# Prompt attention by pairs of heads on row and column halves of the array, with the mask added in VectorE's row reduction

## The chip, the cores and the metric

The kernel runs on one core of one Trainium2 chip. A core has a matrix engine (TensorE, PE in the profile; its weight loads are PEld), a vector engine (VectorE, DVE), a scalar engine (ScalarE, ACT), GpSimd (POOL), SyncE (SP), which issues transfers here, and 16 DMA engines. The metric is the time of one execution on the device in microseconds; lower is better. Before the change three runs took 2658.57, 2660.92 and 2667.46 us.

## The reference, cut to what matters

One step of a hybrid decoder layer over a prompt (1024 tokens) and a sample group (8 sequences of 8 new tokens with 2048 past ones): RMSNorm, one input projection, sparse softmax attention with a token indexer (8 heads of 64), gated DeltaNet (4 heads of 128), output projection, squared-ReLU MLP, final norm. All tensors are float32. The change is in the attention of the prompt:

```
score = sum over indexer heads of relu(qi . ki / 8) * wi, -inf where the key is later than the query
sel   = the 256 highest scores of each query (of its causal keys)
s = q . k / sqrt(64) for the selected keys, else -inf
p = softmax(s);  o = p @ v                     (per head; 8 heads of 64)
```

For queries of the first 256 tokens every causal key is selected.

## The kernel before, in words

The program is a row of stages, each a block in which every engine has its own instruction list, with semaphores between them. Around the change: the indexer and top-256 stages, then the mixer projection, which also turns the top-256 result into masks (one bf16 tile `maskP[t]` of 128 x 128(t+1) per query tile t >= 2, 0 where a key is taken and MASKED = -1e30 elsewhere, L803; `attn_causal` is the causal square, L78) and writes q, scaled by 1/8 (L766), and k transposed to DRAM; conv, gates and the DeltaNet; then `stage_prompt_attention` (L1492), `stage_sample_attention` (L1634), output projection and MLP.

`stage_prompt_attention` works on 64 items, one head h of one query tile t each (t outer, eight heads inner); an item has t+1 key blocks of 128. q, k and v are loaded in three parts (tiles 0 and 1, 2 and 3, 4 to 7) by SyncE, ahead of the first pages for the sample attention; GpSimd loads others of these pages.

The order on each engine is written out by hand:

- TensorE, per item n: `turn(n)`: t+1 transposes of the scaled probabilities into two PSUM banks (L1555); `score(n+2)`: per 512 keys one product of 64 rows (the head's half of the partitions) and one bf16 product of the identity with the mask, which adds the mask in PSUM (L1542, L1544, L1546); `values(n)`: t+1 products with 64 output columns of the array (L1567).
- VectorE: `scale(n+1)`: reciprocal of the row sum and scaling in place (L1619, L1621); `maxes(n+2)`: negated row maximum out of PSUM (L1608); `keep(n)`: the 64 x 128 output of the item into `mix` (L1614).
- ScalarE: copy of the transposed probabilities to SBUF (L1598); `exps(n+2)`: exponential out of PSUM with the row sum (L1588).

Scores of two items lie in four banks, two per item; transposes use two banks, value outputs one each of the last two. A float32 product is two passes, so it is two MATMUL instructions in the trace; a transpose and a bf16 product are one.

Of the kernel before, what the change touches and what calls it, by code (L numbers as in the profile page):

```python
# [58 lines left out]
def constants():  # L59
# [18 lines left out]
    parts["attn_causal"] = MASKED * (col > row)  # L78
# [58 lines left out]
class Kernel:  # L137


    def __init__(self, nc, ctx, a):  # L140
# [28 lines left out]

        self.psI = self.view(m.take(IX_W), IX_W)  # L170
        self.psA = self.view(m.take(3 * AW), 3 * AW)
        self.psC = self.view(m.take(CC), CC)
# [524 lines left out]
def stage_mixer_projection(k):  # L697
# [22 lines left out]
    with nc.Block() as block:  # L720
# [11 lines left out]
        def _(act):  # L732
# [5 lines left out]
            for n, (c, kind, col, wd, at) in enumerate(jobs):  # L738
# [17 lines left out]
                elif c <= V_CHUNK:  # L756
# [9 lines left out]
                    act.activation(stage[i % 4], bank[:, :], ACT.Copy, scale=HD ** -0.5 if c == Q_CHUNK else 1.0).then_inc(kept, 1)  # L766
# [725 lines left out]
def stage_prompt_attention(k):  # L1492
# [6 lines left out]
    m = Map(k.z_at)  # L1499
    prob = [k.view(m.take(SEQ), SEQ) for _ in range(2)]  # L1500
    probT = [k.view(m.take(SEQ), SEQ) for _ in range(2)]
# [3 lines left out]
    items = [(t, h) for t in range(NT) for h in range(H)]  # L1505
# [3 lines left out]
    names = ("scores", "max", "exp", "inv", "scaled", "turned", "kept", "made", "out")  # L1509
    scores, maxed, exped, inverted, scaled, turned, kept, made, out = (k.sem("pa_" + n) for n in names)  # L1510
    n_items = len(items)
    k.stream = PageStream(k)
    with nc.Block() as block:
# [17 lines left out]
        def _(pe):  # L1531
            def score(n):
                t, h = items[n]
                lo = (h % 2) * HD
                if h == 0 and t in first:
                    pe.wait_ge(qk_in[first[t]], 32)
                if n >= 2:
                    pe.wait_ge(exped, n - 1)
                for c in range(0, (t + 1) * P, 512):
                    w = min(512, (t + 1) * P - c)  # L1540
                    bank = k.psum[2 * (n % 2) + c // 512]
                    pe.matmul(bank[:, 0:w], qT[lo:lo + HD, h // 2, t * P:(t + 1) * P], kT[lo:lo + HD, h // 2, c:c + w], start=True, stop=False)  # L1542
                    if t < FIRST_SEL:
                        last = pe.matmul(bank[:, t * P:(t + 1) * P], k.b["ident"], k.b["attn_causal"], start=False, stop=True)  # L1544
                    else:
                        last = pe.matmul(bank[:, 0:w], k.b["ident"], k.maskP[t][:, c:c + w], start=False, stop=True)  # L1546
                last.then_inc(scores, 1)

            def turn(n):
                t, h = items[n]  # L1550
                pe.wait_ge(scaled, n + 1)
                if n:
                    pe.wait_ge(kept, n)
                for j in range(t + 1):
                    last = pe.transpose(k.psum[4 + j // 4][:, (j % 4) * P:(j % 4 + 1) * P], prob[n % 2][:, j * P:(j + 1) * P], k.c["ident"])  # L1555
                last.then_inc(turned, 1)

            def values(n):
                t, h = items[n]
                lo = (h % 2) * HD  # L1560
                if h == 0 and t in first:
                    pe.wait_ge(v_in[first[t]], 16)
                pe.wait_ge(kept, n + 1)
                if n >= 2:
                    pe.wait_ge(out, n - 1)
                for j in range(t + 1):
                    last = pe.matmul(k.psum[6 + n % 2][lo:lo + HD, 0:P], V[:, j, h * HD:(h + 1) * HD], probT[n % 2][:, j * P:(j + 1) * P],  # L1567
                                     start=(j == 0), stop=(j == t))
# [3 lines left out]
            score(1)  # L1572
            for n in range(n_items):
                turn(n)
                if n + 2 < n_items:
                    score(n + 2)
                values(n)

        @block.scalar
        def _(act):  # L1580
            def exps(n):
                t, h = items[n]
                w = (t + 1) * P
                b0 = 2 * (n % 2) * 512
                act.wait_ge(maxed, n + 1)
                if n >= 2:
                    act.wait_ge(turned, n - 1)
                act.activation(prob[n % 2][:, 0:w], k.banks[:, b0:b0 + w], ACT.Exp, bias=stat[:, 0, n:n + 1],  # L1588
                               accum_out=stat[:, 1, n:n + 1]).then_inc(exped, 1)

            exps(0)
            exps(1)
            for n in range(n_items):
                w = (items[n][0] + 1) * P
                act.wait_ge(turned, n + 1)
                if n >= 2:
                    act.wait_ge(made, n - 1)
                act.copy(probT[n % 2][:, 0:w], k.banks[:, 4 * 512:4 * 512 + w]).then_inc(kept, 1)  # L1598
                if n + 2 < n_items:
                    exps(n + 2)  # L1600

        @block.vector
        def _(dve):
            def maxes(n):
                w = (items[n][0] + 1) * P
                b0 = 2 * (n % 2) * 512
# [719 lines left out]
```

## Time and profile before

| | |
|---|---|
| median of three runs | 2660.92 us |
| profiled execution, first to last instruction | 2661.8 us |
| PE busy | 2400.9 us, 90% |
| PEld busy | 1617.1 us, 61% |
| DVE busy | 1399.8 us, 53% |
| ACT busy | 601.4 us, 23% |
| POOL busy | 272.6 us, 10% |

The busy shares are means over the whole program. The page also has the program in 40 slices of 66.5 us; the prompt attention is in the 17th to the 21st. For one stage the stretches, waits and the timeline of that stage are to be read. A matmul's duration includes its way through the array, so durations of matmuls in a row overlap: their pace is read from start to start. "issue" stands for a wait on nothing the profile shows.

### The profile page before, as it was taken

The page shows a single profiled execution, that of the slowest core. Times are in us where ns is not written, and L with a number is a line of the kernel's source. Part 1 is how long each engine was busy: PE and PEld are TensorE (multiplying, and loading weights), DVE is VectorE, ACT ScalarE, POOL GpSimd, SP SyncE. Part 2 cuts the span into 40 slices and gives each one's busy share as a digit, 9 for nine tenths or more (in the row PEclk, how much of TensorE's full clock was granted, in tenths as well). Part 3 has the DMA queues.
Part 4 walks back from the last instruction along what each step waited for, and adds up shares of the span by engine and source line. Part 5 has one row for each costly group of instructions (what it writes and reads, how often), then busy time and mean ns, then how long its engine had stood idle before and what let it go on. Part 6 is the DMA issues. An engine that isn't in the chain of part 4 may idle for free. (4 is left out here: it accounts for less than half of the span.)

```text
span 2661.8 us, 28841 instructions
## 1 busy us (share of the span) xinstructions
PE 2400.9 (90%) x10669; PEld 1617.1 (61%) x10669; DVE 1399.8 (53%) x2208; ACT 601.4 (23%) x1094; POOL 272.6 (10%) x363
## 2 busy tenths in 40 slices
PE   2967999999699987699999999797999999999998
PEld 2522444444258876355654444386888888888887
DVE  3056999999645656534432221265444444444445
ACT  2031442110320101124432111143111211221212
POOL 2221543110020010100000222100000000000000
PEclk9966999999769989559999999898999999999999
DMA  5120001220000001420015674541110110111111
GB/s 142 27 89 1 32 32 48 78 85 12 9 1 1 1 1 33 160 97 1 1 54 180 211 227 128 200 138 53 40 56 32 40 56 32 40 56 32 34 55 68
DMA packets 116152, 171.81 MB, mean 65 GB/s; under 512 B 25784, under 2 KB 66745, under 8 KB 115884
## 3 DMA queue, kind: packets, MB, share of 16 engines
q1 hardware_dynamic: 100140, 124.86, 14.5%
q0 software_dynamic: 15872, 45.11, 5.5%
q8 instruction: 85, 1.39, 0.2%
q14 instruction: 55, 0.45, 0.1%
HBM read 154.02 MB, written 15.91 MB: 64 GB/s over the span
## 5 line engine op out<-in xcount | busy, mean ns | idle before, releaser
L393 PE MATMUL banks<-arena,work 128*128 128x512 f32 x736 | 323.1, 600 | 8.2 <-PEq L292 7.7
L1881 PE MATMUL banks<-h_hi,ml_up_hi 128*128 128x364 f32 (+1 forms) x768 | 253.5, 330 | 8.6 <-DVE ml_up_lo L2217 8.6
L1882 PE MATMUL banks<-h_lo,ml_up_hi 128*128 128x364 f32 (+1 forms) x768 | 253.5, 330 | 0.0
L1883 PE MATMUL banks<-h_hi,ml_up_lo 128*128 128x364 f32 (+1 forms) x768 | 253.4, 330 | 0.0
L393 PEld LDWEIGHTS banks<-arena,work 128*128 128x128 f32 x736 | 140.3, 192 | 186.1 <-issue 186.1
L1881 PE MATMUL banks<-ml_down_hi,ml_hid_hi 128*128 128x512 f32 (+1 forms) x576 | 228.8, 397 | 27.0 <-DVE x L2246 24.5
L524 DVE MATCH_REPLACE8 work<-work 128x384 f32<-128x384 f32 (+6 forms) x224 | 240.0, 1077 | 0.0
L2246 DVE TENSOR_TENSOR x<-x,banks 128x512 f32<-128x512 f32 x256 | 171.5, 685 | 123.3 <-PE banks L1883 123.0
L520 DVE MAX8 work<-work 128x8 f32<-128x384 f32 (+6 forms) x224 | 227.5, 1079 | 0.4 <-PEq L553 0.3
L1882 PE MATMUL banks<-ml_down_lo,ml_hid_hi 128*128 128x512 f32 (+1 forms) x576 | 227.4, 395 | 0.0
L1883 PE MATMUL banks<-ml_down_hi,ml_hid_lo 128*128 128x512 f32 (+1 forms) x576 | 227.0, 394 | 0.0
L2256 DVE TENSOR_TENSOR arena<-arena 128x364 f32<-128x364 f32 (+1 forms) x96 | 51.6, 537 | 209.2 <-ACT arena L2195 209.2
L1881 PEld LDWEIGHTS banks<-h_hi,ml_up_hi 128*128 128x128 f32 x768 | 145.3, 189 | 10.3 <-DVE ml_up_lo L2217 8.8
L1882 PEld LDWEIGHTS banks<-h_lo,ml_up_hi 128*128 128x128 f32 x768 | 145.3, 189 | 0.6
L1883 PEld LDWEIGHTS banks<-h_hi,ml_up_lo 128*128 128x128 f32 x768 | 145.3, 189 | 0.0
L1881 PEld LDWEIGHTS banks<-ml_down_hi,ml_hid_hi 128*128 128x128 f32 (+1 forms) x576 | 106.3, 185 | 58.1 <-DVE x L2246 30.4
L396 PE MATMUL banks<-work,arena 128*128 128x512 f32 (+1 forms) x384 | 124.8, 487 | 0.0
L1883 PEld LDWEIGHTS banks<-ml_down_hi,ml_hid_lo 128*128 128x128 f32 (+1 forms) x576 | 106.3, 185 | 27.0
L1882 PEld LDWEIGHTS banks<-ml_down_lo,ml_hid_hi 128*128 128x128 f32 (+1 forms) x576 | 106.2, 184 | 25.4
L1707 PE MATMUL banks<-work 128*64 128x512 f32 x256 | 116.7, 599 | 0.0
L1542 PE MATMUL banks<-work 64*128 64x512 f32 (+3 forms) x192 | 102.7, 621 | 15.2 <-DMA work<-k_T 15.2
L1743 PE MATMUL banks<-work 128*64 128x512 f32 x256 | 107.7, 611 | 6.9 <-DVE work L1834 6.1
(348 smaller groups left out, 3426.6 us busy)
## 6 DMA issues: line engine op xcount, KB each, us to landing
work<-in_cache_v POOLq DMA_DIRECT2D x128, 256.0 KB, 3.4
work<-in_cache_k SPq DMA_DIRECT2D x128, 256.0 KB, 3.3
arena<-in_w_up SPq DMA_DIRECT2D x32, 512.0 KB, 4.1
arena<-in_w_down SPq DMA_DIRECT2D x32, 512.0 KB, 5.6
work<-in_w_in SPq DMA_DIRECT2D x7, 2048.0 KB, 8.1
op_raw<-in_w_out SPq DMA_DIRECT2D x24, 512.0 KB, 3.5
work<-in_x_prompt SPq DMA_DIRECT2D x8, 512.0 KB, 4.9
x<-in_x_prompt SPq DMA_DIRECT2D x1, 4096.0 KB, 15.3
```

The costliest lines, as they stand in the source:

```text
L393: last = pe.matmul(bank[0:w, :], ring[:, f, col:col + w], hT[:, f, at * 512:(at + 1) * 512], start=(f == 0), stop=(f == KD - 1))
L396: last = pe.matmul(bank[:, 0:w], hT[:, f, at * P:(at + 1) * P], ring[:, f, col:col + w], start=(f == 0), stop=(f == KD - 1))
L520: dve.max(self.best[0:rows, i, :], sc[0:rows, :]).then_inc(self.maxed, 1)
L524: dve.match_replace(sc[0:rows, :], self.best[0:rows, i, :], sc[0:rows, :], TAKEN).then_inc(self.taken, 1)
L1542: pe.matmul(bank[:, 0:w], qT[lo:lo + HD, h // 2, t * P:(t + 1) * P], kT[lo:lo + HD, h // 2, c:c + w], start=True, stop=False)
L1707: last = pe.matmul(rows, qblk[:, (2 * it + b2) * 4 + p, :], kts[n % 2][:, p, :], start=False, stop=(p == 3))
L1743: last = pe.matmul(k.psum[6][b2 * 64:(b2 + 1) * 64, :], PT[:, 4 * c + j, b2 * 64:(b2 + 1) * 64], vp[n % KV_RING][:, j, :], start=(c == 0 a ...
L1881: pe.matmul(out, lh, rh, start=start, stop=False)
L1882: pe.matmul(out, lh, rl, start=False, stop=False)
L1883: return pe.matmul(out, ll, rh, start=False, stop=stop)
L2246: dve.tensor_tensor(part, part, k.psum[4 + n % 4][0:r, :], ALU.add).then_inc(added, 1)
L2256: dve.tensor_tensor(tmp[:, j, 0:w], tmp[:, j, 0:w], tmp[:, j, 0:w], ALU.mult).then_inc(squared, 1)
```

## The change

Heads are taken in pairs, (t, p) with heads 2p and 2p+1. `score` issues, per 512 keys, the product of the even head on rows 0 to 63 and then that of the odd head on rows 64 to 127, into different banks, and no mask product. q is projected with the negated scale and the prompt's masks have the other sign, so scores and masks are negated. VectorE's `mask` adds scores and mask, writes the sum to the SBUF probability tile and takes the row minimum, in one `tensor_tensor_reduce`. ScalarE takes the exponential with scale -1, in place in SBUF. Transposes go to a ring of three banks in chunks of up to 512 keys (banks 4 to 6), each chunk with its own copy on ScalarE. `values` alternates the two heads of the pair on the two column halves, into one bank (7), of which one VectorE copy of 128 x 128 takes both heads. Scores have two sets of banks up to 512 keys, and one set above.

There are as many probability tiles (`prob`) as before, two, but they are now the two heads of one pair, and a pair has no second set; the transposed ones (`probT`) have two sets. `prob` moves over buffers that are done with by then.

```diff
-    parts["attn_causal"] = MASKED * (col > row)
+    parts["attn_causal"] = -MASKED * (col > row)
...
-  act.activation(stage[i % 4], bank[:, :], ACT.Copy, scale=HD ** -0.5 if c == Q_CHUNK else 1.0).then_inc(kept, 1)
+  act.activation(stage[i % 4], bank[:, :], ACT.Copy, scale=-HD ** -0.5 if c == Q_CHUNK else 1.0).then_inc(kept, 1)
...
-  dve.tensor_scalar(masks[i][0:rows, :], sc[0:rows, :], TAKEN, MASKED, ALU.not_equal, ALU.mult)
+  dve.tensor_scalar(masks[i][0:rows, :], sc[0:rows, :], TAKEN, MASKED if i == k.topk.sample else -MASKED, ALU.not_equal, ALU.mult)
...
+    def score_at(n, e):
+        return 512 * (2 * (n % 2) + e if width(n) <= 512 else 2 * e)
...
+            def score(n):                                        # TensorE
+                t, p = pairs[n]
                 ...
+                if width(n) > 512:
+                    pe.wait_ge(masked, 2 * n)
+                elif n >= 2:
+                    pe.wait_ge(masked, 2 * (n - 1))
+                for c in halves(n):
+                    w = min(512, width(n) - c)
+                    for e in range(2):
+                        lo, at = e * HD, score_at(n, e) + c
+                        last = pe.matmul(k.banks[:, at:at + w], qT[lo:lo + HD, p, t * P:(t + 1) * P], kT[lo:lo + HD, p, c:c + w],
+                                         start=True, stop=True)
                 last.then_inc(scores, 1)
+            def turn(n):
+                for e in range(2):
+                    pe.wait_ge(scaled, 2 * n + e + 1)
+                    for c in halves(n):
+                        u = chunk_of[n, e, c]
+                        if u >= NB:                              # NB = 3
+                            pe.wait_ge(kept, u - NB + 1)
+                        for at in range(c, min(c + 512, width(n)), P):
+                            last = pe.transpose(k.psum[4 + u % NB][:, at - c:at - c + P], prob[e][:, at:at + P], k.c["ident"])
+                        last.then_inc(turned, 1)
+            def values(n):
                 ...
+                pe.wait_ge(kept, last_chunk(n, 1) + 1)
                 if n:
+                    pe.wait_ge(out, n)
                 for j in range(t + 1):
+                    for e in range(2):
+                        h = 2 * p + e
+                        last = pe.matmul(k.psum[7][e * HD:(e + 1) * HD, 0:P], V[:, j, h * HD:(h + 1) * HD], probT[n % 2][e][:, j * P:(j + 1) * P],
+                                         start=(j == 0), stop=(j == t))
             score(0)
+            for n in range(n_pairs):
+                if n + 1 < n_pairs:
+                    score(n + 1)
+                turn(n)
+                if n:
+                    values(n - 1)
...
+            def exps(n, e):                                      # ScalarE
+                i, w = 2 * n + e, width(n)
+                act.wait_ge(masked, i + 1)
+                act.activation(prob[e][:, 0:w], prob[e][:, 0:w], ACT.Exp, scale=-1.0, bias=stat[:, 0, i:i + 1],
+                               accum_out=stat[:, 1, i:i + 1]).then_inc(exped, 1)
+            def keep_turned(n):
                 if n >= 2:
                     act.wait_ge(made, n - 1)
+                for e in range(2):
+                    for c in halves(n):
+                        u, w = chunk_of[n, e, c], min(512, width(n) - c)
+                        act.wait_ge(turned, u + 1)
+                        act.copy(probT[n % 2][e][:, c:c + w], k.psum[4 + u % NB][:, 0:w]).then_inc(kept, 1)
                 # order: exps(0, 0), exps(0, 1), then per n: keep_turned(n), exps(n + 1, 0), exps(n + 1, 1)
...
+            def mask(n, e):                                      # VectorE
                 ...
                 dve.wait_ge(scores, n + 1)
+                if n:
+                    dve.wait_ge(turned, last_chunk(n - 1, e) + 1)
+                dve.tensor_tensor_reduce(out=prob[e][:, 0:w], in0=k.banks[:, at:at + w], in1=mask_of[t], scale=1.0, scalar=3.0e38,
+                                         op0=ALU.add, op1=ALU.min, accum_out=stat[:, 0, i:i + 1]).then_inc(masked, 1)
...
+            for n in range(n_pairs):
+                if n + 1 < n_pairs:
+                    for e in range(2):
+                        mask(n + 1, e)
+                    for e in range(2):
+                        scale(n + 1, e)
+                if n:
+                    keep(n - 1)
```

`scale` is as before, with one index per head of a pair. The masks of tiles 0 and 1 are laid out by three small VectorE instructions at the start of the stage.

## Rows read from the trace of the kernel before

**Rows 1.** The page's 40 slices: TensorE's granted clock in tenths of full speed.
```profile
PEclk9966999999769989559999999898999999999999
```

**Rows 2.** Busy times by stretch: length, engines (instructions), clock, DMA share, GB/s.
```profile
1112.44:1127.70 15.26, 14.48 (x44) 8.18 (x45) 7.13 (x30) 5.46 (x23) 6.95 (x13) 0.50 1.03 377
...
1151.50:1185.50 34.00, 34.00 (x93) 16.92 (x91) 11.14 (x32) 9.09 (x24) 0.00 (x0) 0.50 0.00 0
1185.50:1198.70 13.20, 13.20 (x37) 6.71 (x37) 4.07 (x11) 3.40 (x8) 0.00 (x0) 0.50 0.00 1
...
1322.30:1372.10 49.80, 47.26 (x270) 29.84 (x269) 20.04 (x34) 18.64 (x25) 0.00 (x0) 1.00 0.00 1
```

**Rows 3.** Waits in 1100 to 1372 us: who, for whom, total us, times, longest.
```profile
ACT work L1588 <- DVE work L1608: 139.2, 64, 5.1
...
DVE work L1608 <- PE banks L1546: 81.9, 48, 2.6
...
PE banks L1542 <- DMA work<-k_T: 15.2, 1, 15.2
```

**Rows 4.** Timeline of an item of tile 7: start, length, instruction, idle before.
```profile
1340.34 1.11 ACT L1588 ACTIVATE work<-banks,work 128x1024 f32<-128x1024 f32 x1 [3.00 <-DVE work L1608]
...
1340.86 1.09 PE L1555 MATMUL banks<-arena,work 128*128 128x128 f32 x8
...
1341.35 0.19 ACT L1588 ACTIVATION_READ_ACCUMULATOR work<-banks,work 128x1 f32 x1
1341.58 0.16 DVE L1619 RECIPROCAL work<-work 128x1 f32<-128x1 f32 x1 [0.31 <-ACT work L1588]
1341.78 0.75 DVE L1621 TENSOR_SCALAR work<-work 128x1024 f32<-128x1024 f32 x1
...
1341.89 1.12 PE L1542 MATMUL banks<-work 64*128 64x512 f32 x2
...
1342.94 0.39 PE L1546 MATMUL banks<-work,arena 128*128 128x512 bf16 x1
...
1343.26 1.12 PE L1542 MATMUL banks<-work 64*128 64x512 f32 x2
...
1344.64 1.96 PE L1567 MATMUL banks<-work 128*64 128x128 f32 x16
1344.74 1.22 DVE L1608 TENSOR_REDUCE work<-banks 128x1 f32<-128x1024 f32 x1 [2.21 <-PE banks L1546]
...
1346.53 1.09 PE L1555 MATMUL banks<-arena,work 128*128 128x128 f32 x8
```

**Rows 5.** A VectorE group by shape, whole program: busy us, mean ns, idle before.
```profile
L1279 DVE TENSOR_TENSOR arena<-arena,banks 128x1024 f32<-128x1024 f32 x20 | 24.5, 1223 | 11.3 <-PE banks L1187 11.3
```

**Rows 6.** Timeline of the indexer's first products, and of one score product of tile 6.
```profile
131.30 1.56 PE L472 MATMUL banks<-work 64*128 64x384 f32 x8 [0.83 <-PEq L411]
...
1300.87 0.91 PE L1542 MATMUL banks<-work 64*128 64x384 f32 x2
```

**Rows 7.** Timeline in the sample indexer stage: products on column quarters, and one beside.
```profile
188.15 0.20 PEld L592 LDWEIGHTS banks<-work 64*32 64x32 f32 x8 [1.57 <-ACT work L623]
188.15 1.93 PE L592 MATMUL banks<-work 64*32 64x512 f32 x8 [1.16 <-ACT work L623]
...
190.96 1.97 PE L598 MATMUL banks<-work,arena 128*64 128x512 f32 x2 [0.87 <-DVE work L648]
```

**Rows 8.** The stage's groups of 512 columns by shape: busy us, mean ns.
```profile
L1588 ACT ACTIVATE work<-banks,work 128x512 f32<-128x512 f32 x8 | 5.5, 688 | 15.8 <-DVE work L1608 15.8
...
L1598 ACT COPY work<-banks 128x512 f32<-128x512 f32 x8 | 4.7, 584 | 2.6 <-PE banks L1555 2.1
L1621 DVE TENSOR_SCALAR work<-work 128x512 f32<-128x512 f32 x8 | 3.9, 487 | 0.3
```

**Rows 9.** DMA issues of the v parts: KB each, us from issue to landing.
```profile
work<-out_new_v_prompt SPq DMA_DIRECT2D x2, 512.0 KB, 13.6
...
work<-out_new_v_prompt SPq DMA_DIRECT2D x1, 1024.0 KB, 20.0
```

More of the change, by code:

```diff
@@ L1504, in stage_prompt_attention @@
     mix = k.view(k.hT_at, KD, TOK)
-    items = [(t, h) for t in range(NT) for h in range(H)]
+    pairs = [(t, p) for t in range(NT) for p in range(H // 2)]
     parts = [(0, 2 * P), (2 * P, 4 * P), (4 * P, SEQ)]
@@ L1532, in score @@
             def score(n):
-                t, h = items[n]
-                lo = (h % 2) * HD
-                if h == 0 and t in first:
+                t, p = pairs[n]
+                if p == 0 and t in first:
                     pe.wait_ge(qk_in[first[t]], 32)
[L1537 to L1546, printed above, removed]
+                if width(n) > 512:
+                    pe.wait_ge(masked, 2 * n)
+                elif n >= 2:
+                    pe.wait_ge(masked, 2 * (n - 1))
@@ L1569, in values @@
                 last.then_inc(made, 1)
             score(0)
-            score(1)
-            for n in range(n_items):
+            for n in range(n_pairs):
+                if n + 1 < n_pairs:
+                    score(n + 1)
                 turn(n)
-                if n + 2 < n_items:
-                    score(n + 2)
-                values(n)
+                if n:
+                    values(n - 1)
+            values(n_pairs - 1)
         @block.scalar
         def _(act):
[L1581 to L1589, printed above, removed]
@@ L1610, in keep, with scale @@
+            def scale(n, e):
+                i, w = 2 * n + e, width(n)
+                dve.wait_ge(exped, i + 1)
+                dve.reciprocal(stat[:, 2, i:i + 1], stat[:, 1, i:i + 1]).then_inc(inverted, 1)
+                dve.wait_ge(inverted, i + 1)
+                dve.tensor_scalar(prob[e][:, 0:w], prob[e][:, 0:w], stat[:, 2, i:i + 1], None, ALU.mult).then_inc(scaled, 1)
             def keep(n):
-                t, h = items[n]
-                lo = (h % 2) * HD
+                t, p = pairs[n]
@@ L1623, in _ @@
-            maxes(0)
-            maxes(1)
-            scale(0)
-            for n in range(n_items):
-                if n + 1 < n_items:
-                    scale(n + 1)
-                if n + 2 < n_items:
-                    maxes(n + 2)
-                keep(n)
+                dve.tensor_copy(mix[:, p, t * P:(t + 1) * P], k.psum[7][:, 0:P]).then_inc(out, 1)
+            dve.tensor_copy(mask_of[0], k.b["attn_causal"]).then_inc(laid, 1)
+            dve.memset(mask_of[1][:, 0:P], 0.0).then_inc(laid, 1)
@@ new lines, in _ @@
+            dve.tensor_copy(mask_of[1][:, P:2 * P], k.b["attn_causal"]).then_inc(laid, 1)
+            for e in range(2):
+                mask(0, e)
+            for e in range(2):
+                scale(0, e)
+            for n in range(n_pairs):
+                if n + 1 < n_pairs:
+                    for e in range(2):
+                        mask(n + 1, e)
+                    for e in range(2):
+                        scale(n + 1, e)
+                if n:
+                    keep(n - 1)
```

69 lines of the change are left out of this document (30 added, 39 removed).

## The prediction

> **What bounds the kernel now.** I read the slices of the page first: in the 17th and 18th, where the prompt attention begins, TensorE's granted clock dips to five tenths, the low level [rows 1]. The busy times by stretch then cut the stage at its query tiles: it runs from 1112.44 to 1372.10 us, 259.7 us, and from 1127.7 on TensorE has no idle microsecond up to the last tile, whose 49.8 us hold 47.3 busy ones; VectorE is busy for 11.1 of 34.0 us in tile 2 and for 20.0 of 49.8 in tile 7 [rows 2]. Up to 1198.7, within tile 3, the granted clock is 0.5 (1.2 GHz), although TensorE always had work; from there it is 1.0 (2.4 GHz). The waits show who is late: VectorE waits 81.9 us for score products, ScalarE 139.2 us for the row maximum, TensorE's one long wait is the 15.2 us for the first k part [rows 3]. So TensorE's own work is the stage's time, and every microsecond taken off it counts until something else is late.
>
> The timeline of one head of tile 7 prices it [rows 4]. Eight transposes run from 1340.86 to 1341.89 (1.03), a 512-column score product takes 1.05 and the mask's product behind it 0.32 (1342.94 to 1343.26), twice each (2.75), the 16 passes of the value product 1.89: 5.67 per head, 11.3 per pair. A change from one kind of tile to another leaves a bubble of about 0.1, seen as 1.03 for transposes whose pace inside is 0.11.
>
> **The mask.** It leaves TensorE and joins the row reduction. At tile 7 that is 4 x 0.32 = 1.3 us less per pair on TensorE. On VectorE the new two-input instruction replaces a reduction that takes 1.22 for 1024 columns [rows 4]. No row shows it. Its nearest row is a two-input VectorE instruction that reads PSUM, 1.22 for the same size [rows 5]; from below the bound is 1.22, because the same columns are read; from above, two instructions' worth, 2.45. I take 1.25, near that row, since inputs and output stream are the same and only the minimum is added. The negated scale and masks cost nothing: same instructions, other constants. Three small copies of masks stand ahead of the loop, in VectorE's 15 us wait for the first scores.
>
> **The scores by row halves.** The two heads of a pair now stand next to each other on different row halves. The trace has that pattern: the indexer's four 64-row products of 384 columns, heads alternating between the halves, take 1.56 together at the full clock; one such product alone takes 0.91 in this stage [rows 6]. So they overlap, and more than halve the time per product, as the second pass's weight load is also covered. For 512 columns: 1.56 x 512 / 384 = 2.08, less 0.2 of tail after the last start, gives 1.9 for the four products of a tile-7 pair, where 4.2 stood. If the halves took turns it would be 4.2 again.
>
> **The values by column halves.** Here the heads of a pair alternate between the 64-column halves, all 128 rows in use. The nearest row: at the low clock four 512-column products on four column quarters take 1.93, and one product with 64 columns takes 1.97 beside them [rows 7]. So column parts do run together, into one bank as here. But those are 64 rows deep and long. If it holds, a tile-7 pair costs 16 rounds of 0.118 = 1.9 instead of 3.8; the other end is 3.8. I take 1.9.
>
> The Trainium skill speaks against this (TensorE: Matmul & The Clock Gate, The mechanism): it says that a weight load overlaps running matmuls only where the row group differs, and both heads use all rows here. In [rows 7] the eight weight loads of four column quarters on the same rows take 0.20 in all, which agrees with a load per quarter side by side, but they stand ahead of the matmuls and so don't refute it. By that rule the sum would be the one of rival B.
>
> **TensorE's new work per pair.** With b = t + 1 blocks of 128 keys: scores, transposes and values at tile 7 are 1.9 + 2 x 1.03 - 0.1 + 1.9 = 5.75. At the low clock tile 2 (b = 3) costs: scores about 1.6 (a low-clock 384-column product is twice 0.84 to the next start, the second beside it), transposes 1.7, values 1.5: 4.8. Tiles 0 and 1 would be 1.8 and 3.1.
>
> **The ring that is late next.** There is one probability buffer per head of the pair, and ScalarE serves both. Once ScalarE has copied the last transposed chunk of head 1 of pair n, it does the two exponentials of pair n+1, VectorE scales head 1, TensorE transposes it, ScalarE copies it: that is one turn. With 1.21 for an exponential and its accumulator read at 1024 columns (1340.34 to 1341.54), 0.98 for reciprocal and scaling, 0.64 until the first transposed half has landed, 0.58 for a copy of 512 columns, and some 0.15 for hand-overs [rows 4, 8]: tile 7 is 2 x 1.21 + 0.98 + 0.64 + 2 x 0.6 + 0.15 = 5.4, under TensorE's 5.75. For 512 columns: 2 x 0.78 + 0.73 + 0.64 + 0.6 + 0.15 = 3.7 (tile 3), and between them 4.3, 4.6 and 5.0 for tiles 4 to 6, against TensorE's 3.6 to 4.9. The masking instructions lie beside it: the one of head 0 starts when its transposes are done, and is over before ScalarE's copies are. The score product of the pair after next must wait for both maskings where scores fill two banks each (tiles 4 to 7), and comes between value product and transposes: I add 0.1 to 0.3 for such collisions.
>
> So, per pair: tile 0 3.5 (2.5 and the pipeline's first fill of 4 us over four pairs), tile 1 3.5 (3.1 and a wait between the two heads' transposes), tile 2 4.8, tile 3 3.8, tiles 4 to 7 4.4, 4.9, 5.3 and 5.75. The sum is 35.95, times four pairs 143.8 us.
>
> The loads don't end up late: tile 2 would start near 1112.4 + 28 = 1140, and its 512 KB parts, which SyncE issues ahead of the last ones, need 13.6 us at the median to land [rows 9]; the last v part needs 20.0, the DMA share is 0 from 1151.5 on [rows 2], so by then all is in, and tile 4 would start near 1112.4 + 62 = 1174. The next stage's first pages are in by then too, so that it begins as before.
>
> **The sum.** 259.7 - 143.8 = 115.9 us saved against the profiled execution's 2661.8: 2545.9. Its span is that time, first to last instruction, and lies 0.9 above the median of the timed runs, 2660.92, so I leave it: 2546.
>
> **The clock.** I let it stay low through tiles 0 to 2 and rise at tile 3, as before. It could rise a tile earlier: 6 less. It could rise a tile later: 8 more. TensorE will be idle for parts of each ring in tiles 3 to 6, which it wasn't.
>
> **Rivals.**
> A, the forecast: both halves overlap, new instruction near 1.25, clock high from tile 2, 3 or 4 on. 2535 to 2560. For it: [rows 6, 7]. Chance 0.68.
> B, one part doesn't give: the value halves take turns (2 b x 0.109 more per pair at the high clock, twice that at the low one, less the 0.1 to 0.8 that the ring hides: 15 us for tiles 3 to 7 and 11 for tiles 0 to 2, 2572), or the masking instruction costs 2.45 at 1024 columns (VectorE's 2 x 2.45 + 2 x 0.98 + 0.3 = 7.2 is then tile 7's bound; by the line in E it comes to 155 us and the ring's waits, up to 173: 2575), or the score halves take turns (some 40 us, 2586). Against it: the rows of each pattern. Chance 0.17.
> C, the clock stays low, or falls back whenever the ring lets TensorE idle. TensorE's work then doubles, 1.3 b + 0.5 per pair: 10.9 at tile 7. The sum over tiles 1 to 7 is 49.0, with tile 0 52.5, times four 210: 2612 if throughout. For it: the low clock from before 1112 to 1198.7 with TensorE never idle [rows 2]. Against it: the indexer stretch of [rows 6] has idle gaps at the full clock, and the array is now filled in both halves. The Trainium skill (the same page, HAM oscillation) tells of kernels whose short idles between groups of matmuls take them back to the low clock; by it this rival would be the likely one, and [rows 6] shows a stretch where that didn't happen. Chance 0.09.
> D, the change doesn't do what it says: neither kind of half overlaps, only the mask is gone. TensorE's pair is then 11.3 - 1.3 less two bubbles, 9.8 at tile 7, and the stage is 0.87 of what it was, 225: 2627. Chance 0.03.
> E, slower than before: the masking instruction works off its columns several times slower than the rows of its kind. It stands twice in every pair with everything else behind it. At k times the row's price, put as 0.155 + 0.133 b (1.22 at b = 8; the fixed part an estimate, a little under the 0.22 that scaling's 0.75 and 0.487 at 1024 and 512 columns leave at none [rows 4, 8]), VectorE's pair is 2 k (0.155 + 0.133 b) + 1.23 + 0.13 b with scaling and copy; over b = 1 to 8 that is 12.1 k + 14.6, and the four pairs reach 259.7 at k = 4.2, or 5.1 us for 1024 columns: from there it decides. At k = 5 the stage is 300: 2702. For it: no row shows the instruction. Against it: the two-input row and the reduction both take 1.22 for 1024 columns, scaling 0.75 [rows 4, 5]. Chance 0.03.
>
> **How the numbers follow.** Predicted is A's 2546. The range leaves out the ends of B, C, D and E: 2530 (clock earlier and smaller collisions) to 2588. About 0.3%, 8 us, is what a measurement tells from no change; A to D are faster by far more, E is slower: faster 0.96, same 0.01, slower 0.03.
>
> **What would show it.** Stage length near 144 us, from first score product to last copy. Four 512-column products of a pair of tile 7 in about 1.9, the 32 value passes in about 1.9 with starts in twos; the masking row at about 1.25 for 1024 columns. A tile-5 pair every 4.9 us with TensorE waiting for ScalarE's copy or VectorE's scaling; a tile-7 pair every 5.75 with TensorE nearly full. Granted clock 1.0 from tile 3 at the latest, and through. I would be wrong by B if value starts stand 0.11 apart, by C if 0.5 shows in tiles 4 to 7, by E if VectorE is busy throughout.

## The result and the profile after

The changed kernel takes 2529.43 us (median of 4, 2528.99 to 2531.76) against 2661.44 of the kernel before on the same chip: ratio 0.9506, 95% interval 0.9484 to 0.9527. The forecast was 2546, in a range of 2530 to 2588. So the sign came out, and of the mechanism all but the clock; the gain was 17 us larger than forecast. The median lies 0.6 us below the low end, which is less than the interval can tell.

The page of the kernel after has two rows to set beside those of before, the span and the slices of the granted clock:

```profile
span 2527.2 us, 28652 instructions
PEclk9975999999968998959999998989999999999999
```

Where [rows 1] have two slices at five tenths in this stage, one is left, from 1074 to 1137 us (the other five, in the fourth slice, belongs to an earlier stage). Busy times by stretch, cut at the start of head 0's exponential in each tile's first pair, answer to [rows 2] (length; then busy time and number of instructions of TensorE, its weight loads, VectorE, ScalarE and GpSimd; then granted clock, DMA share and GB/s):

```profile
1110.74:1121.08 10.34, 8.66 (x40) 4.72 (x40) 6.41 (x37) 5.24 (x25) 4.82 (x10) 0.50 1.04 376
1121.08:1131.24 10.16, 9.61 (x60) 4.90 (x60) 8.06 (x37) 6.84 (x24) 2.02 (x4) 0.80 1.03 384
1131.24:1143.13 11.89, 10.83 (x86) 5.90 (x84) 9.86 (x37) 8.65 (x25) 0.00 (x0) 1.00 1.04 383
1143.13:1157.01 13.88, 13.33 (x114) 8.12 (x112) 11.43 (x37) 10.26 (x26) 0.00 (x0) 1.00 0.24 84
1157.01:1173.89 16.88, 15.71 (x144) 10.76 (x142) 13.30 (x37) 12.10 (x33) 0.00 (x0) 1.00 0.01 2
1173.89:1192.60 18.71, 18.40 (x174) 12.69 (x172) 14.85 (x37) 13.85 (x33) 0.00 (x0) 1.00 0.00 1
1192.60:1213.47 20.87, 20.87 (x198) 14.43 (x196) 16.16 (x37) 15.55 (x33) 0.00 (x0) 1.00 0.01 2
1213.47:1230.55 17.08, 17.08 (x166) 12.05 (x164) 13.35 (x28) 12.95 (x26) 0.00 (x0) 1.00 0.00 1
1230.55:1239.76 9.21, 7.32 (x104) 6.22 (x100) 3.57 (x9) 4.54 (x9) 0.00 (x0) 1.00 0.01 3
sum 129.02, PE 121.81 PEld 79.80 DVE 96.99 ACT 89.98 POOL 6.83; mean PE 13.53 PEld 8.87 DVE 10.78 ACT 10.00 POOL 0.76
```

The rows run through tiles 0 to 6, then the first three pairs of tile 7, then its last pair with the drain, the work that is left when no further pair follows. The stage is 129.0 us long where it was 259.7. TensorE has no idle time in tile 6 and tile 7's first pairs and loses about a microsecond in tile 4. What no row of before foretold is the clock column: 0.5 in tile 0, 0.80 in tile 1, 1.00 from tile 2 on. The granted clock changes at 1125.2, 14.5 us after the first score product; in the kernel before it rose 86 us after it.

The timeline of tile 7 in the kernel after, TensorE's rows of two pairs, beside the two-head piece that [rows 4] show:

```profile
1220.18 1.99 PE L1562 MATMUL banks<-work 64*128 64x512 f32 x8
1222.09 2.04 PE L1574 MATMUL banks<-arena,work 128*128 128x128 f32 x16
1224.07 1.97 PE L1587 MATMUL banks<-work 128*64 128x128 f32 x32
1225.96 1.99 PE L1562 MATMUL banks<-work 64*128 64x512 f32 x8
1227.88 2.04 PE L1574 MATMUL banks<-arena,work 128*128 128x128 f32 x16
```

From start to start: scores 1.91, transposes 1.98, values 1.89, together 5.78 for two heads where they took 11.3. Eight 64-row passes of 512 columns in 1.91 and 32 value passes in 1.89 mean that both kinds of half run side by side; in the trace the single value passes start in twos, 6 to 7 ns apart. One turn of VectorE and ScalarE in the same kernel, from tile 6 into tile 7:

```profile
1212.15 1.23 DVE L1635 CUSTOM_DVE_ANT_0 work<-banks,work 128x1024 f32<-128x1024 f32 x1 [0.84 <-PE banks L1574]
...
1213.30 0.08 DVE L1635 DVE_READ_ACCUMULATOR2_ANT work<- 128x1 f32 x1
1213.30 1.22 DVE L1635 CUSTOM_DVE_ANT_0 work<-banks,work 128x1024 f32<-128x1024 f32 x1
1213.47 1.18 ACT L1605 ACTIVATE work<-work 128x1024 f32<-128x1024 f32 x1
```

The masking instruction, L1635, costs 1.22 us for 1024 columns, what the plain reduction cost in [rows 4], and 0.08 for the read of its accumulator. The waits of tiles 4 to 6 in the kernel after (engine, line, waited for: total us, times, longest) answer to [rows 3]:

```profile
ACT work L1615 <- PE banks L1574: 15.0, 12, 1.6
...
DVE work L1635 <- PE banks L1574: 5.7, 13, 0.8
DVE work L1641 <- ACT work L1605: 4.2, 12, 0.4
PEld banks L1574 <- ACT work L1615: 4.0, 12, 0.7
```

ScalarE and VectorE wait for TensorE's transposes. TensorE's weight loads are held once per pair, a third of a microsecond, when the next chunk of transposes needs the bank that ScalarE is copying (L1615).

### The profile page after: what moved, and what is told of

The parts are those of the page before. It is cut to its first block and busy times, and to the rows that moved or that the text cites. A ratio compares the mean times of both kernels' runs of the same rounds, so it can differ in the third digit from the quotient of the medians.

```text
span 2527.2 us, 28652 instructions
## 1 busy us (share of the span) xinstructions
PE 2259.2 (89%) x10573; PEld 1545.3 (61%) x10573; DVE 1387.6 (55%) x2243; ACT 598.1 (24%) x1126; POOL 271.8 (11%) x363
## 5 line engine op out<-in xcount | busy, mean ns | idle before, releaser
L526 DVE MATCH_REPLACE8 work<-work 128x384 f32<-128x384 f32 (+6 forms) x224 | 246.5, 1284 | 0.0
L522 DVE MAX8 work<-work 128x8 f32<-128x384 f32 (+6 forms) x224 | 233.8, 1278 | 0.4 <-PEq L555 0.3
L1485 POOL DMA_DIRECT2D work<-in_cache_v x128 | 69.1, 539 | 393.5 <-issue 392.3
```

What stands on the lines that cost most here:

```text
L522: dve.max(self.best[0:rows, i, :], sc[0:rows, :]).then_inc(self.maxed, 1)
L526: dve.match_replace(sc[0:rows, :], self.best[0:rows, i, :], sc[0:rows, :], TAKEN).then_inc(self.taken, 1)
L1485: q.dma_start(ring[n % KV_RING][:, p, :], src).then_inc(sems[n % KV_RING], 16)
```

## The experiments

Open after the result were: what makes the clock rise two tiles earlier, and what each part is worth. Three causes were set against each other: the paired score products, which fill the rows of both halves; the value products of both heads side by side; the mask's products gone from TensorE. "Stage" is first score product to last copy of a profile. Each kernel's ratio is to the kernel before on the same chip, with its 95% interval. Unless said otherwise the edit is to the kernel after.

**Score products one behind the other.** A one-column product on all rows stands between the two heads' products.

```diff
                         last = pe.matmul(k.banks[:, at:at + w], qT[lo:lo + HD, p, ...
-                                         start=True, stop=True)
+                                         start=True, stop=False)
+                        last = pe.matmul(k.banks[:, at:at + 1], k.b["ident"], k.b["attn_causal"][:, 0:1], start=False, stop=True)
```

> Behind each score product a one-column product on the whole array that adds zero is issued, so that the two heads' row halves can't run side by side; all else is the changed kernel, whose stage takes 129.0 us and whose clock rises in tile 1. A tile-7 pair should cost TensorE 5.7 + 2.45 (4.2 instead of 1.75 for the scores) + 0.4 for the four insertions = 8.5 us instead of 5.7. Theory H (the clock rose two tiles early because the paired score products fill both row halves): it now rises in tile 3 or later, and the stage takes 185 to 200. Rival V (because the value halves run side by side) and rival M (because the mask products and their switches are gone): it still rises in tile 1 or 2, and the stage takes 165 to 178. If the row halves never mattered, the stage stays under 140.

2606.71 us, ratio 0.9783 (0.9757 to 0.9810); stage 203.8 us, 75 more. Its timeline in tile 7:

```profile
1290.89 0.18 PE L1565 MATMUL banks<-arena 128*128 128x1 bf16 x1
1291.00 1.12 PE L1562 MATMUL banks<-work 64*128 64x512 f32 x2
1292.06 0.18 PE L1565 MATMUL banks<-arena 128*128 128x1 bf16 x1
1292.16 1.13 PE L1562 MATMUL banks<-work 64*128 64x512 f32 x2
```

The product alone takes 1.06, near the 1.05 of the kernel before, and 1.16 to the next with its separator. Its busy times by stretch:

```profile
1140.00:1177.00 37.00, 37.00 (x134) 19.22 (x134) 14.74 (x52) 13.41 (x36) 0.00 (x0) 0.50 0.22 70
1177.20:1194.00 16.80, 16.34 (x106) 8.90 (x104) 9.49 (x29) 7.67 (x18) 0.00 (x0) 1.00 0.01 1
1250.00:1293.00 43.00, 43.00 (x270) 25.18 (x270) 20.96 (x45) 20.58 (x40) 0.00 (x0) 0.92 0.00 1
```

The clock stays at 0.5 for 66 us of a busy TensorE and rises at 1177.1, in tile 3 as before. So the paired scores are what moves it. They are also the largest part. The separators themselves are an estimated 96 x 0.11 = 11 us at the high clock, somewhat more at the low one, of the 75. The stage came out above the 185 to 200 expected. After the rise the clock falls back five times, for 3.4 us each, and each time during, or within 0.3 us behind, a run of 64-row products alone that had lasted three microseconds or more: the last fall is at 1293.2, and its run starts at 1288.68; the timeline above shows the end of it. Not every such run is followed by a fall.

**Value passes one head behind the other.**

```diff
-                for j in range(t + 1):
-                    for e in range(2):
+                for e in range(2):
+                    for j in range(t + 1):
```

> The value products are issued head by head (all key blocks of the even head, then of the odd one) instead of alternating; all else as changed. If side-by-side work needs neighbours in the queue, a tile-7 pair costs 1.75 more, 7.4 us instead of 5.7. Theory H: the clock still rises in tile 1 or 2, stage 150 to 156. Rival V: it rises in tile 3, stage near 166. If the queue finds the other head's products by itself, nothing changes: 129.

2540.62 us, ratio 0.9545 (0.9530 to 0.9561); stage 145.4. Its timeline in tile 7:

```profile
1235.75 3.33 PE L1587 MATMUL banks<-work 128*64 128x128 f32 x32
1239.01 1.99 PE L1562 MATMUL banks<-work 64*128 64x512 f32 x8
1240.93 2.04 PE L1574 MATMUL banks<-arena,work 128*128 128x128 f32 x16
```

3.26 to the next start instead of 1.89. That is less than the 3.8 that two heads took before, so the stage stays under the 150 to 156 expected. The clock rises at 1124.7, as after: the value halves are worth 16 us of the stage, and taking them away does not delay the rise.

**Both apart**, the two edits together.

> Both of the former edits together: pairs of heads and the mask on VectorE as changed, but no halves side by side. This is rival D of the prediction with the insertions' cost on top: stage 215 to 240, a tile-7 pair near 10.3 us, the clock up in tile 3 by theories H and V, in tile 1 by M. The whole should then be within 1.5% of the kernel before or 1% faster, which would say that the halves bring nearly the whole gain.

2620.88 us, ratio 0.9840 (0.9821 to 0.9859); stage 215.2, 86 more than after, less than the 75 and 16 of the parts. The stage is still 44.5 us shorter than before, of which the mask's products are 32 (the next experiment). The clock rose at 1156.1, in tile 2 and 21 us earlier than with the scores alone apart. I had not expected that order. The timelines ahead of the two rises, first both apart, then scores apart:

```profile
1152.04 1.52 PE L1576 MATMUL banks<-arena,work 128*128 128x128 f32 x6
1153.49 2.03 PE L1589 MATMUL banks<-work 128*64 128x128 f32 x12
1155.45 1.19 PE L1562 MATMUL banks<-work 64*128 64x384 f32 x2
...
1172.95 1.95 PE L1576 MATMUL banks<-arena,work 128*128 128x128 f32 x8
1174.83 1.55 PE L1589 MATMUL banks<-work 128*64 128x128 f32 x12
1176.31 1.50 PE L1562 MATMUL banks<-work 64*128 64x512 f32 x2
```

Both rises come just behind a stretch of transposes and values, all on 128 rows, of 3.41 and 3.36 us. With scores alone apart the stretches of tile 2 are 2.9 us at most. Values in turn take longer, and so the first long stretch comes a tile sooner. This fits the order, but no run tests it. Later on the clock fell back five times, for 3.4 or 6.8 us, each time during or just behind a run of 64-row products alone, as in the kernel with scores apart.

**The kernel before without its mask products.** The edit is to the kernel before, whose masking is left out.

```diff
-                    pe.matmul(bank[:, 0:w], qT[...], kT[...], start=True, stop=False)
-                    if t < FIRST_SEL:
-                        last = pe.matmul(bank[:, t * P:(t + 1) * P], k.b["ident"], k.b["attn_causal"], ...)
-                    else:
-                        last = pe.matmul(bank[:, 0:w], k.b["ident"], k.maskP[t][:, c:c + w], ...)
+                    last = pe.matmul(bank[:, 0:w], qT[...], kT[...], start=True, stop=True)
```

> The kernel before without its mask products (no mask is applied in the prompt's attention, so its output leaves the masking out); all else as before. TensorE saves 0.33 us per 512 columns at the full clock: the stage falls from 259.7 to 228 to 238. Rival M: the clock rises in tile 0, 1 or 2 instead of tile 3 (stage then 205 to 225). Theory H and V: it rises in tile 3 as before or later.

2626.51 us, ratio 0.9870 (0.9853 to 0.9886); stage 227.5, 32.2 less than before. Its busy times by stretch:

```profile
1150.00:1195.00 45.00, 45.00 (x125) 24.37 (x125) 15.92 (x45) 13.17 (x33) 0.00 (x0) 0.50 0.00 1
1195.20:1240.00 44.80, 44.80 (x253) 29.56 (x252) 26.06 (x58) 21.82 (x43) 0.00 (x0) 1.00 0.00 1
```

The rise is at 1195.2, in tile 3 as before (1198.7), with no idle microsecond ahead of it. The mask's products, gone, do not lift the clock. This kernel has no separators, so these are not what keeps the clock low with scores apart. This is also rival D's arithmetic by itself, the old work less the mask: 227.5 against the 225 and 2626.5 against the 2627 that D was given. Built as D describes it, in pairs without overlap, it is the kernel with both apart: 215.2 with some 11 us of separators in it, so D's 225 was too high there.

**Scores and values apart in tiles 0 and 1 only**, where the clock rises.

```diff
-                                         start=True, stop=True)
+                                         start=True, stop=not (t < 2))
+                        if t < 2:
+                            last = pe.matmul(k.banks[:, at:at + 1], k.b["ident"], k.b["attn_causal"][:, 0:1], start=False, stop=True)
...
+                order = [(j, e) for j in range(t + 1) for e in range(2)] if t >= 2 else [(j, e) for e in range(2) for j in range(t + 1)]
```

> The changed kernel, with the one-column separation of the score halves and the head-by-head value order in tiles 0 and 1 alone. It asks what a low clock would have cost tile 2, where the prediction had it. By theory H the clock can't rise before tile 2, so tile 2 begins low: its pairs take 4.6 to 4.8 us instead of 2.97 until the clock rises, within tile 2 after some pairs; the stage takes 129 + 4 x 0.5 + 4 x 2 + 3 to 7 = 142 to 147. If tile 2's pairs take 3.0 at the low clock as well, the clock was not what the prediction mis-sized. If the clock rises in tile 1 all the same, theory H falls.

2537.20 us, ratio 0.9531 (0.9511 to 0.9551); stage 138.3. Its busy times by stretch:

```profile
1125.00:1142.80 17.80, 17.80 (x73) 9.69 (x72) 9.17 (x41) 8.20 (x29) 0.38 (x1) 0.50 1.04 385
1142.81:1160.00 17.19, 16.00 (x119) 8.78 (x120) 14.35 (x51) 12.16 (x33) 0.00 (x0) 1.00 0.28 92
```

TensorE is full and the clock low until the pairing begins with tile 2, whose first scores start at 1138.97; 3.8 us later it is high. That ties the rise to the pairing in time, and not to how far into the stage it is. The stage is shorter than the 142 to 147 expected, since tile 2 ran at the high clock almost throughout (2.97 per pair). So this run doesn't price a low clock in tile 2; a later one does.

**Add and minimum as two instructions.**

```diff
-                dve.tensor_tensor_reduce(out=prob[e][:, 0:w], ... op0=ALU.add, op1=ALU.min, accum_out=...)
+                dve.tensor_tensor(prob[e][:, 0:w], k.banks[:, at:at + w], mask_of[t], ALU.add).then_inc(added, 1)
+                dve.wait_ge(added, i + 1)
+                dve.tensor_reduce(stat[:, 0, i:i + 1], prob[e][:, 0:w], AX_X, ALU.min).then_inc(masked, 1)
```

> VectorE adds the mask and takes the row minimum in two instructions (an addition into the probability tile, then a reduction over it) instead of one. The fused one takes 1.22 us at 1024 columns, of which the mask adds nothing to the former reduction. With two, VectorE's pair at tile 7 is 4 x 1.22 + 2 x 0.95 + 0.3 = 7.1 us against TensorE's 5.7, and it gates the ring: 7.1 to 7.5 per tile-7 pair, stage 160 to 172. Rival: the second reduction hides beside ScalarE's copies (VectorE waits 0.4 to 0.8 us before each masking): stage 135 to 145.

2572.97 us, ratio 0.9663 (0.9642 to 0.9684); stage 176.6, 47.6 more. Its groups by shape (busy us, mean ns):

```profile
L1636 DVE TENSOR_TENSOR work<-banks,work 128x1024 f32<-128x1024 f32 x8 | 9.8, 1220 | 6.2 <-PE banks L1575 6.2
L1638 DVE TENSOR_REDUCE work<-work 128x1 f32<-128x1024 f32 x8 | 9.8, 1220 | 0.3
```

1.22 each: the fused one costs as much as either alone, and the second is on the path. Rival B's price for that, 2575, came out within 2 us, but in part by luck. Its bound of 7.2 per tile-7 pair measured 9.7, with VectorE busy for only 20.2 of 27.4 us in tile 7's first three pairs: the masking waits for transposes, and these for scaling. The stage is over B's highest value of 173 and over the 160 to 172 expected of this run, and the rest of the program was 5.6 us shorter. TensorE now idles 1.9 to 3.0 us at a time in tiles 6 and 7, and the clock falls back for 3.4 us at a time, five times inside the stage.

**Products in TensorE's idle time ahead of the stage**, to raise the clock sooner: 16 at the end of the stage before, 8 ahead of the first pair's scores, while TensorE waits for q and k.

```diff
             turn(NT)                # end of the stage before
+            for _ in range(16):
+                pe.matmul(k.psum[6][:, 0:P], k.c["ident"], k.c["ident"], start=True, stop=True)
...
+            for _ in range(8):
+                pe.matmul(k.psum[6][:, 0:P], k.c["ident"], k.c["ident"], start=True, stop=True)
             score(0)
```

> Sixteen 128-column products on the whole array, whose result nobody reads, at the end of the stage before and eight more while TensorE waits for the first q and k; all else as changed. TensorE is idle there for 10 and 5 us. If the low clock in tiles 0 and 1 costs what the rows say (first copy late, 2.3 and 2.5 per pair against a ring of about 2.0 and 2.5), the clock is high from tile 0 on and the stage is 1 to 4 us shorter, 125 to 128. Rival: tiles 0 and 1 are bound by the ring and nothing moves; or the clock is low again by the first score, since q and k come 5 us later.

2527.70 us, ratio 0.9491 (0.9472 to 0.9511); stage 129.1: as after. The clock was high from 1099.1 to 1105.9, low again, and rose at 1126.4.

**More of them**, 22 and 20.

> As warm_start, with 22 products at the end of the stage before and 20 while TensorE waits for q and k, so that it isn't idle before the first score (in warm_start the clock was high at 1099.1 to 1105.9 and low again at the first score). If the low clock costs tile 0 nothing because its ring bounds it, tile 0's pairs stay at 2.1 to 2.3 and tile 1's first at 2.5 instead of 2.73: stage 128. If it costs, tile 0 falls to 1.8 to 2.0 per pair, stage 127. Either way under 3 us of the whole, at the edge of what times can tell; the trace decides. If the 20 products run at the low clock they end 8.5 us after the stage's start and delay the first score by 3: stage as before, whole 3 longer.

2536.87 us, ratio 0.9529 (0.9516 to 0.9542). Its busy times by stretch:

```profile
1098.90:1105.70 6.80, 3.81 (x34) 3.62 (x33) 0.00 (x0) 0.00 (x0) 0.00 (x0) 1.00 0.90 288
1112.55:1119.38 6.83, 4.51 (x38) 3.22 (x37) 3.32 (x20) 2.96 (x14) 3.23 (x6) 1.00 1.04 376
1119.38:1126.20 6.82, 6.45 (x30) 2.94 (x28) 4.85 (x24) 3.70 (x17) 3.25 (x6) 0.50 1.04 383
```

High within tile 0, then low again until 1126.2. Tile 0's first two pairs took 1.99 each instead of 2.13, while the first score product came 3.3 us later; the stage is 128.4 us. The other 4.7 us by which the whole is longer lie behind the stage and have no cause in the edit. Warming ahead of the stage doesn't pay here.

**ScalarE head by head** instead of pair by pair: a shorter path from one head's copy to its exponential.

```diff
-                keep_turned(n)
-                if n + 1 < n_pairs:
-                    exps(n + 1, 0)
-                    exps(n + 1, 1)
+                for e in range(2):
+                    keep_turned(n, e)
+                    if n + 1 < n_pairs:
+                        exps(n + 1, e)
```

> ScalarE takes copies and exponential head by head (copies of head 0, exponential of head 0 of the next pair, copies of head 1, exponential of head 1) instead of all copies and then both exponentials; all else as changed. If the ring through ScalarE (two exponentials, scaling, transposes, copies) bounds tiles 3 to 6 at 3.47, 4.22, 4.68 and 5.22 us, these fall towards TensorE's own 3.0, 3.7, 4.3 and 4.9, and the stage by 5 to 8 us, to 121 to 124. Rival: ScalarE stands before head 0's exponential for the masking of VectorE while copies are ready, and the pairs get longer by up to 0.5: stage 130 to 140.

2532.29 us, ratio 0.9512 (0.9496 to 0.9528); stage 134.3, 5 us longer. Waits of its stage:

```profile
DVE work L1640 <- ACT work L1605: 21.2, 40, 1.1
ACT work L1605 <- DVE work L1634: 17.8, 30, 5.1
```

ScalarE's exponential now waits for VectorE's masking, and VectorE's reciprocal for the exponential, where in the kernel after the latter wait is 12.4 us in the stage. By the stage the change's order was the better one; the intervals of the whole times overlap.

**Tile 2 at the low clock.** TensorE is held for 12.4 us by fills on GpSimd ahead of tile 2's third pair.

```diff
+            pool.wait_ge(out, 8)
+            for i in range(32):
+                if i:
+                    pool.wait_ge(held, i)
+                pool.memset(k.view(k.psI_at + 192, 204), 0.0).then_inc(held, 1)
...
+                if n == 10:
+                    pe.wait_ge(held, 32)
```

> The changed kernel, with TensorE held for about 10 us before the third pair's scores of tile 2, by 32 small writes of GpSimd one after the other that TensorE waits for. It prices a low clock in tile 2, which no run shows with the halves side by side: in the hold the clock falls, and the one or two pairs behind it run low. Expected by the prediction's own term: about 4.8 us per pair at the low clock, against 2.97 at the high one. If the term was too high as tile 1's was (3.5 forecast, 2.73 seen), a low-clock pair takes 3.9 to 4.1. Then the clock rises again within 4 to 8 us of work (theory H). If a pair takes 3.0 at the low clock, the clock costs nothing here.

A single execution, 2541.88 us. TensorE's rows of its timeline, the first with the wait for GpSimd behind it:

```profile
1147.55 1.65 PE L1570 MATMUL banks<-work 64*128 64x384 f32 x4 [12.44 <-POOL work L1552]
1149.13 1.54 PE L1582 MATMUL banks<-arena,work 128*128 128x128 f32 x6
...
1150.60 1.55 PE L1595 MATMUL banks<-work 128*64 128x128 f32 x12
...
1152.08 1.10 PE L1570 MATMUL banks<-work 64*128 64x384 f32 x4
```

The clock is 0.5 from 1138.9 to 1152.5, so this pair runs at the low one: 1152.08 - 1147.55 = 4.53 us. At the high clock a tile-2 pair takes 2.97. The rise in tile 1 came at 1128.6 in this execution (1125.2 in the kernel after), so three tile-1 pairs ran wholly or mostly at the low clock: 2.73, 2.82 and 3.03.

**The mask's products put back** beside the masking instruction.

```diff
+                    for e in range(2):
+                        at = score_at(n, e) + c
+                        ...
+                        last = pe.matmul(k.banks[:, at:at + w], k.b["ident"], k.maskP[t][:, c:c + w], start=False, stop=True)
```

> The changed kernel, with the mask products on TensorE put back behind each pair of score products, on top of VectorE's addition (the mask is added twice, which changes nothing for a softmax). It prices the part of the change that takes the mask off TensorE. A 512-column bf16 product costs 0.32 with its switch in the kernel before, some 0.22 where several follow each other: a tile-7 pair takes 4 x 0.22 + 0.1 = 1.0 more, 6.7 us. Tiles 5 to 7 have TensorE full and pay it all (0.8, 0.9, 1.0 per pair), tiles 3 and 4 half of it: stage 129 + 4 x 3.3 = 142. If the masks cost as before (0.32 each), 147. If TensorE were not the bound in tiles 5 to 7, under 134.

2552.38 us, ratio 0.9586 (0.9571 to 0.9600); stage 145.6, 16.6 more; tile-7 pairs 6.8. The clock rises at 1124.5, as after. That is over the 142 expected and under the 147 of the old price. In the new arrangement, where TensorE's pair is the bound, the four products of 512 columns cost 1.1 a pair.

**Even chunks in tiles 4 and 5**: 384 and 256 columns, and twice 384, instead of 512 and the rest.

```diff
+    step = lambda n: 512 if width(n) <= 512 else (pairs[n][0] + 2) // 2 * P
+    cuts = lambda n: range(0, width(n), step(n))
-            for c in halves(n):
+            for c in cuts(n):
```

> The changed kernel with tile 4's probabilities turned and copied in chunks of 384 and 256 instead of 512 and 128, and tile 5's in 384 and 384 instead of 512 and 256. In tiles 4 and 5 the pair's fourth chunk of transposes waits 0.4 to 0.5 for ScalarE's copy of the first, whose bank it needs. With a first chunk of 384 that copy is over 0.2 earlier: tile 4 from 4.22 to 4.0, tile 5 from 4.68 to 4.5 per pair, stage 127 to 128. If ScalarE's own sum (four copies and two exponentials) is the ring, nothing moves: 129.

2524.58 us, ratio 0.9486 (0.9473 to 0.9499); stage 128.4: pairs of 4.12 and 4.59 instead of 4.22 and 4.68, 0.8 us over the two tiles. The whole is the lowest measured, but the interval overlaps that of the kernel after, and only 0.8 us of it has a place.

## Why the prediction was right in kind and short in size

The pairs' starts give each tile's time beside the forecast:

| tile | forecast per pair | measured per pair | stage, measured less forecast |
|---|---|---|---|
| 0 | 3.5 (2.5 and fill) | 2.26 and 1.3 of fill in all | -3.7 |
| 1 | 3.5 | 2.54 | -3.8 |
| 2 | 4.8 | 2.97 | -7.3 |
| 3 | 3.8 | 3.47 | -1.3 |
| 4, 5, 6 | 4.4, 4.9, 5.3 | 4.22, 4.68, 5.22 | -1.9 |
| 7 | 5.75 | 5.70, the last one 9.2 | +3.3 |

Together 14.8 us less than the 143.8 forecast. Outside the stage the profiled execution is 3.9 shorter (2661.8 - 259.7 against 2527.2 - 129.0), and the median lies 2.2 above the profiled span: 16.6 in all. The 3.9 is not a term: the rest of the program took from 2392 to 2405 us in the kernels here whose edits lie in this stage alone. So whether the time falls just inside or just outside the range is chance; the 14.8 of the stage is not.

**The step that failed** is the clock: "I let it stay low through tiles 0 to 2 and rise at tile 3, as before." It rose in tile 1. Tile 2, forecast at 4.8 per pair, took 2.97, which is 7.3 us and half of the stage's miss. The price at the low clock was nearly right, 4.8 against 4.53 with the clock held down, so 6.2 of the 7.3 are the state of the clock and 1.1 its price. The prediction had this step beside its forecast ("a tile earlier: 6 less") and left it out of the sum. I had read [rows 2] as "low although always busy" and carried it over as a matter of place. What it showed was low with score products on half the rows. With the pairing withheld the low clock lasts into tile 3 (scores apart), with the pairing withheld in two tiles it lasts as long as they do. Without the values' pairing it still rises in tile 1, and the kernel before without its mask products still in tile 3. The prediction had the clue, "the array is now filled in both halves", and used it only against a fall of the clock. How the chip weighs the rows in use stays open: the falls behind 64-row products alone and the rises behind 128-row work fit it, but a pairing that changes nothing else in the order was not run.

**The terms that were mis-sized.** Tile 0's fill, 4 us for 1.3; why it is so short was not tested. A tile-1 pair at the low clock, 3.5 for 2.73 (2.73 to 3.03 where the low clock lasted longer), of which 0.4 was a wait that does not show. The end, the other way: I priced tile 7's last pair like the others, but nothing runs beside its exponentials and it has two value products behind it; 9.2 for 5.75. That drain is a term that I left out.

**What held.** TensorE's tile-7 pair of 5.75 measured 5.70, from 1.9, 1.95 and 1.9 that measured 1.91, 1.98 and 1.89. The masking instruction of 1.25 measured 1.22 and 0.08. The rings of tiles 3 to 6 came within 0.1 to 0.3 per pair, with TensorE full from tile 6 on. The loads were in, the DMA share being 0.24 in tile 3 and 0.01 from there. Of the rivals, D's arithmetic came out with the mask alone gone, but not in pairs without overlap (215.2 for 225), and the second case of B met its price in part by luck. B's value case came to 16 us, near its 15 for tiles 3 to 7; of its 11 for tiles 0 to 2 nothing showed (pairs of 2.28, 2.54 and 3.00 there, for 2.26, 2.54 and 2.97). C's low clock in tiles 4 to 7 and E's slow instruction did not show.

The rule of the Trainium skill that I set against the value halves (TensorE: Matmul & The Clock Gate, The mechanism: a weight load overlaps a running product only if it targets other rows) does not hold in this trace. Both heads' loads use all 128 rows, each its own half of the columns, and two passes start every 0.118 us, where in turn one takes 0.102. The measurement decides.

The same page of the Trainium skill, under A second HAM failure mode, says that frequent short idles between groups of products make the clock swing. That is the rule behind rival C; the section that the prediction named for it, HAM oscillation, tells of waits for data. With two masking instructions the clock does swing, at idles of 1.9 to 3.0 us, which agrees. With scores apart it also falls, in a stretch where TensorE has no idle microsecond (43.00 of 43.00 us busy, clock 0.92), which idles can't explain.

## What to carry to other kernels

When a stretch runs at the low clock although TensorE is always busy, look at how many rows its products use before treating the clock as a matter of place: here pairing 64-row products gave the scores in less than half their time (1.91 for 4.2 us) and the high clock two tiles sooner. Price the last item of a pipeline by itself, since nothing overlaps it. When a reduction reads a score tile anyway, a two-input reduction can take a mask along for nothing (here 1223 ns for 1220), and removes a product on TensorE without a second pass on VectorE.

## What the runs showed that I had not expected

- TensorE, busy nearly throughout, stayed at the low clock for 66 us (scores apart) and 83 us (no mask) with 64-row products in turn, and left it within 15 us with the pairs.
- Ten times the clock fell during or just behind a run of 64-row products alone, with under 0.5 us of idle time in TensorE (five times with scores apart, five with both apart).
- The fused add and minimum costs 1223 ns for 1024 columns, as the add or the reduction alone, 291 ns for 128, and 83 ns for its accumulator.
- Column halves with all rows in use overlap their weight loads: 32 passes in 1.97 us, in turn 3.33.
- At 1.16 per separated product against 0.48 per paired one, a one-column product between two that could overlap more than doubles them.
